# The even mixer's attention output made by feature: values stand in the array, GpSimd scales the probabilities

## The reference, cut to what matters

```python
def even_mixer(x, w_in, w_uk, w_uv, b_f, w_o, rel_bias):
    ...
    # latent heads (a): keys chosen by the indexer, at most 128 of those up to the query
    la = einsum('bthr,btkr->bhtk', ql, c_sel) + bias
    pa = jax.nn.softmax(la, axis=-1)
    oa = einsum('bhtk,btkr->bthr', pa, c_sel)
    ...
    # forgetting heads (b)
    lb = einsum('bthd,bshd->bhts', qb, k_b) + cum_f(query) - cum_f(key)
    pb = jax.nn.softmax(where(causal, lb, -inf), axis=-1)
    ob = einsum('bhts,bshd->bthd', pb, v_b)
    ...
    o_a = einsum('bshr,hrd->bshd', oa, w_uv).reshape(bsz, seq, 512)
    return concatenate([o_a, ob], axis=-1) @ w_o
```

## Time and profile before

| | us |
|---|---|
| median of 3 runs | 1915.85 (1915.56 to 1916.55) |
| the profiled execution | 1915.55, its span 1913.5 |
| TensorE busy | 1871.7 (98%) |
| VectorE, ScalarE, GpSimd busy | 928.1, 727.5, 386.2 |
| even mixer, units under way | about 772 to 952 |

### The profile page before, as it was taken

How to read it: one execution, slowest core, us unless ns; L and a number is a source line. 1 busy time by engine, 2 the same in 40 slices (tenths; PEclk the granted TensorE clock), 3 DMA queues, 4 the chain that set the end, 5 groups by cost and what they waited for, 6 DMA issues and landing times.

```text
span 1913.5 us, 23337 instructions
## 1 busy us (share of the span) xinstructions
PE 1871.7 (98%) x9766; PEld 1543.6 (81%) x9766; DVE 928.1 (49%) x1501; ACT 727.5 (38%) x1223; POOL 386.2 (20%) x224
## 2 busy tenths in 40 slices
PE   7999988999999999999999999999989999999998
PEld 6788977888888888777788888888768898888886
DVE  5675544322322234776555555523543366556334
ACT  5664434322322243556734334321323244344211
POOL 1433433111110034211031111100254421111000
PEclk9999989999999999999999999999999999999999
DMA  5211032232233232110022322332322322322321
GB/s 198 69 53 67 7 120 81 88 103 95 90 109 110 80 136 69 67 42 26 23 82 95 101 98 89 118 113 78 110 88 87 112 78 99 108 91 91 119 99 66
DMA packets 28764, 170.01 MB, mean 89 GB/s; under 512 B 3386, under 2 KB 5602, under 8 KB 10866
## 3 DMA queue, kind: packets, MB, share of 16 engines
q1 hardware_dynamic: 28660, 168.53, 25.4%
HBM read 166.37 MB, written 2.11 MB: 88 GB/s over the span
## 4 chain that ended last, share of the span: by engine, by line
PE 93%; DVE 3%; ACT 2%; POOL 1%; issue 0%; DMA 0%; SPq 0%; ACTq 0%; DVEq 0%
PE ps L572 27%; PE ps L573 27%; PE ps L574 27%; PE ps L1112 2%; PE ps L1040 1%; PE ps L1075 1%; PE ps L1079 1%; PE ps L1097 1%; POOL wL L2494 1%; PE ps L652 1%; ACT wH L1281 1%; PE ps L702 1%; PE ps L856 0%; PE ps L865 0%; DVE hL L1819 0%; PE ps L1051 0%
## 5 line engine op out<-in xcount | busy, mean ns | idle before, releaser
L572 PE MATMUL ps<-hH,wH 128*128 128x512 f32 (+1 forms) x1568 | 603.3, 385 | 5.4 <-POOL wL L2494 1.9
L574 PE MATMUL ps<-hH,wL 128*128 128x512 f32 (+1 forms) x1568 | 591.1, 377 | 0.0
L573 PE MATMUL ps<-hL,wH 128*128 128x512 f32 (+1 forms) x1568 | 591.0, 377 | 0.0
L1812 DVE TENSOR_TENSOR wL<-raw,wH 128x1024 fp32r<-128x1024 f32 (+1 forms) x196 | 240.3, 1265 | 331.5 <-ACT wH L1281 331.5
L1281 ACT ACTIVATE wH<-raw 128x1024 fp32r<-128x1024 f32 (+2 forms) x298 | 290.2, 1023 | 282.5 <-PE ps L574 282.5
L2494 POOL TENSOR_TENSOR wL<-raw,wH 128x1024 fp32r<-128x1024 f32 (+2 forms) x102 | 246.4, 2438 | 689.8 <-ACT wH L1281 689.8
L572 PEld LDWEIGHTS ps<-hH,wH 128*128 128x128 f32 x1568 | 296.1, 189 | 66.6 <-issue 5.5
L574 PEld LDWEIGHTS ps<-hH,wL 128*128 128x128 f32 x1568 | 295.8, 189 | 54.4
L573 PEld LDWEIGHTS ps<-hL,wH 128*128 128x128 f32 x1568 | 296.1, 189 | 52.3 <-issue 1.4
L572 PE MATMUL ps<-wH,aH 128*128 128x512 f32 x528 | 209.0, 396 | 0.0
L574 PE MATMUL ps<-wH,aL 128*128 128x512 f32 x528 | 208.8, 395 | 0.0
(11 more groups left out here) (370 smaller groups left out, 1918.8 us busy)
## 6 DMA issues: line engine op xcount, KB each, us to landing
raw<-in_wbig SPq DMA_DIRECT2D x139, 1024.0 KB, 4.8
rows<-in_rows SPq DMA_DIRECT2D x12, 512.0 KB, 5.8
x<-in_x SPq DMA_DIRECT2D x8, 512.0 KB, 5.7
raw<-in_wbig SPq DMA_DIRECT2D x8, 512.0 KB, 3.6
out<-x SPq DMA_DIRECT2D x4, 512.0 KB, 2.6
near<-u_scratch SPq DMA_DIRECT2D x1, 1024.0 KB, 7.3
raw<-in_wbig SPq DMA_DIRECT2D x1, 1000.0 KB, 8.1
raw<-in_wbig SPq DMA_DIRECT2D x1, 600.0 KB, 10.7
```

Of the source, the lines that this page charges most:

```text
L572: e.matmul(o, hi, m_hi, start=first, stop=False)
L573: e.matmul(o, hi, m_lo, start=False, stop=False)
L574: return e.matmul(o, lo, m_hi, start=False, stop=end)
L1812: e.tensor_tensor(wL[r][:, cs], raw[r][:, cs], wH[r][:, cs].bitcast(F32), ALU.subtract).then_inc(*low_dve.one(c, h))
```

## The change

The value product is turned round: the 64 columns of values stand in the array, and the 128 queries of a block of `Pt` are streamed. Its result has the features of one head on 64 partitions (the lower half for even heads, the upper for odd ones) and the queries along the columns. ScalarE copies it without a scale to `oTb` or `oTa`, which already have the layout of `hH`. The scale, one number a query, is now applied before the transpose: VectorE's reciprocal follows its exponential in the same iteration, and GpSimd multiplies the probabilities by it (a new strand `units` on GpSimd), and the transpose waits for that. No transposes of the output are left. Seven of its eight tiles are rounded and subtracted in seven F steps (`OUT_TILES`), the eighth, tile 3, in four parts during the output product. The order string is another one. On VectorE the wait for the earlier unit's output copy before a score's maximum is gone, and GpSimd's copies for the indexer come one step later.

```diff
 def even_order():
-    return ("FFFFFIFFFFFFFFFFFFFFFFFFFFFIFFFFFFFFFFFFFFFFIFFFFFFFIFIFFIFIFIFIFIFIFFFIFFIIFFIIIIFFFFIIFFFFIFIIFAFIFFFIIIFFIFFIAFAFFAIA"
-            "AAAIAAFAIAAIAFAFIAIFFIAIFAAAAFFAAIAAFIAAIFAAIAAIAIFAIFAAAFAIFIFAIFFFFIIAAIAIAFFIAFAFAAIFFAAIAAIAFFAIFFIAFIAFAIAAFAFIAFAI"
-            "AFAIAIIAAFAAIFIFFAIAAFFIAAAFFFFFAAFFIAIAAAFIAAFIAIFFIFAAIAAAFIIAAFAFIAFAAAAIAAIAFIAAIFAIAAFIAAAAAIAAAAAIAAAFAAAAIAAAAAFI"
-            "AFAAFAIAAAAIAAAAAAAFAFIAAAAFAIAAAAAIAAAAIAAAAAAAAAAIAAAAAAAAAAIAAAAAAAFAAAAFAAAFAAFA")
+    return ("FFFFFFFFFFFFFFFFFFFFFFFFFIFFFFFFFFIFFFFFFFFFIFFFFFFFIFIFIFIFIFIFIFIIFFIFFFFIIIFFFFFIFFFIIFIFIIFFFAFIFIAFAFIFIFAAIIFFAIFF"
+            "FAIFAAIAFAAIAAAIFAIAAIIFAAFFFFAFAIIAAAIAAIAFAAFFAIAFAIIAFFAAFIAIAAIIAFFIFAAFAFFAIIIIFFIAFIAAFIFAIAAIAAIAAIAAFFAIAIAFFAFI"
+            "AAAIFAAAIFAFFIAFIFFAFFAFIAIFFAAAAIAAFAFAIAFFAAIAFAAIFIAAFIIIIFAFIAAAFFAIFFAIAAAIAAIAAIAAIFAAFAAIAAAAAAAAIAAFFAAIAAAAAAAA"
+            "AIAFFAIAAAAAAAAAAIAFFAAIAAAAAAAAIFAAAIAAAAAAIAAAFAIAAIAAAAAAFAAAAAAAAAAAAAAAAAAFAAFFAFF")
...
         cf = R("cf", [8, 2, 512])
-        otb = R("otb", [128, 4, 512])
+        oTb = R("oTb", [128, 4, 512])
         sco = R("sco", [128, 512])
...
         va = R("va", [128, 4, 512])
-        ota = R("ota", [128, 4, 512])
+        oTa = R("oTa", [128, 4, 512])
         sel_at = [0, 0, 256, 640]
...
             "row", "x_again", "ones_q", "ones_k", "CM", "wuk", "wuv", "anti", "far", "near", "cum_q", "cum_k", "sgg", "sgw", "sgb", "out")}
-        pre, ev, gate, att, ssd, gdn0, gdn1, sums, mix, res, ffn, even, idx, unit, lat, odd, sgu, ln = stages = [
+        pre, ev, gate, att, ssd, gdn0, gdn1, sums, mix, res, ffn, even, idx, unit, lat, heads, odd, sgu, ln = stages = [
             Marks(sem, n) for n in ("pre", "evac", "gate", "att", "ssd", "gdn0", "gdn1", "sums", "mix", "res", "ffn", "even", "index",
-                                    "unit", "latent", "odd", "sgu", "norm")]
+                                    "unit", "latent", "heads", "odd", "sgu", "norm")]
         gdn = (gdn0, gdn1)
...
-            def turn_b(i):
-                turn("mix", i, otb[:, i, :], [unit.act.at("o", 28 + i)], (1,), i % 2)
-            def turn_a(i):
-                turn("mix", i, ota[:, i, :], [unit.act.at("o", 60 + i)], (0,), 4 + i)
             def dense_even():
...
                     yield from feat(C_QA + j, [0, 1], "res", lambda t: [even.act.at("qa", 2 * j + t)])
-                for i in range(4):
-                    turn_b(i)
+                for k in OUT_TILES:
                     yield
...
                         clear(b)
-                        w.wait_ge(*unit.act.at("exp", n + 1))
+                        w.wait_ge(*unit.pool.at("scaled", n + 1))
                         for j in range(i + 1):
...
                         for j in range(i + 1):
-                            t = e.matmul(ps[6][:, 0:64], Pt[n % 2][:, 128 * j:128 * j + 128], v[:, j, 64 * h:64 * h + 64], start=j == 0, stop=j == i)
+                            t = e.matmul(ps[6][64 * (h % 2):64 * (h % 2) + 64, 0:128], v[:, j, 64 * h:64 * h + 64], Pt[n % 2][:, 128 * j:128 * j + 128], start=j == 0, stop=j == i)
                         t.then_inc(*unit.pe.one("o", n))
...
             def of_mixed(k, i):
-                return [turned_lo.at("mix", i, k // 4)]
-            turn3 = ln_stage(0, [63, 64], [65, 66], hH, hL, of_mixed, True, {i: lambda i=i: turn_a(i) for i in range(4)})
+                return [heads.dve.at("last", i) if k == 3 else heads.dve.at("lo", k)]
+            turn3 = ln_stage(0, [63, 64], [65, 66], hH, hL, of_mixed)
             conv_ffn(0, turn3)
...
         def conv_start(n):
-            return [sgu.dve.at("lo", 7)] if n else [turned_pe.at("mix", 3, 0)]
+            return [sgu.dve.at("lo", 7)] if n else [heads.dve.at("last", 3)]
+        OUT_TILES = [4, 5, 6, 7, 0, 1, 2]
+        def oT(k):
+            return (oTa if k < 4 else oTb)[:, k % 4, :]
+        def out_unit(k):
+            return (32 if k < 4 else 0) + 8 * (k % 4) + 7
...
-            if tag == "mix":
-                return [prod.at(62, 1)]
             return {"first": [], "xn": [prod.at(16, i)], "res": [prod.at(50, i)], ("ln", 0): [prod.at(66, i)],
...
                         yield from feat_side(c, split, even_tile(c))
-                for i in range(4):
-                    turn("mix", i, (1,), i % 2)
-                    yield
-                yield "done"
+                for k in OUT_TILES:
+                    w.wait_ge(*prod.at(62, 1))
+                    w.wait_ge(*unit.act.at("o", out_unit(k)))
+                    e.activation(hH[:, k, :], oT(k), ACT.Copy).then_inc(*heads.act.one("hi", k))
+                    yield
+                yield "done"
+            def last_high(i):
+                w.wait_ge(*prod.at(62, 1))
+                w.wait_ge(*unit.act.at("o", 60 + i))
+                e.activation(hH[:, 3, 128 * i:128 * i + 128], oT(3)[:, 128 * i:128 * i + 128], ACT.Copy).then_inc(*heads.act.one("last", i))
...
                         h, i = n % 32 // 4, n % 4
+                        r = slice(64 * (h % 2), 64 * (h % 2) + 64)
                         w.wait_ge(*unit.pe.at("o", n))
-                        w.wait_ge(*unit.dve.at("rec", n))
                         if n >= 32:
                             w.wait_ge(*unit.pe.at("score", 31))
-                        o = ota if n >= 32 else otb
-                        e.activation(o[:, i, 64 * h:64 * h + 64], ps[6][:, 0:64], ACT.Copy, scale=sx2[:, n % 4, 2:3]).then_inc(*unit.act.one("o", n))
+                        o = oTa if n >= 32 else oTb
+                        e.activation(o[r, h // 2, 128 * i:128 * i + 128], ps[6][r, 0:128], ACT.Copy).then_inc(*unit.act.one("o", n))
                         yield
...
-            turn3 = ln_stage(0, [63, 64], [65, 66], True, {i: lambda i=i: turn("mix", i, (0,), 4 + i) for i in range(4)})
+            turn3 = ln_stage(0, [63, 64], [65, 66], True, {i: lambda i=i: last_high(i) for i in range(4)})
             conv_ffn(0, turn3)
...
                         yield from feat_side(c, split, even_tile(c))
-                for i in range(4):
-                    turn("mix", i, (1,), i % 2)
-                    yield
-                yield "done"
+                for k in OUT_TILES:
+                    w.wait_ge(*heads.act.at("hi", k))
+                    e.tensor_tensor(hL[:, k, :], oT(k), hH[:, k, :].bitcast(F32), ALU.subtract).then_inc(*heads.dve.one("lo", k))
+                    yield
+                yield "done"
+            def last_low(i):
+                s = slice(128 * i, 128 * i + 128)
+                w.wait_ge(*heads.act.at("last", i))
+                e.tensor_tensor(hL[:, 3, s], oT(3)[:, s], hH[:, 3, s].bitcast(F32), ALU.subtract).then_inc(*heads.dve.one("last", i))
...
                         w.wait_ge(*unit.pe.at("score", u))
-                        for p in [idx.pe.at("widx"), idx.act.at("ln"), idx.dve.at("negcum")] if u < 4 else [unit.pe.at("turn", u - 4), unit.act.at("o", u - 4)]:
+                        for p in [idx.pe.at("widx"), idx.act.at("ln"), idx.dve.at("negcum")] if u < 4 else [unit.pe.at("turn", u - 4)]:
                             w.wait_ge(*p)
...
                         yield
+                    if 0 <= n + 2 < 64:
+                        s = (n + 2) % 4
+                        w.wait_ge(*unit.act.at("exp", n + 2))
+                        e.reciprocal(sx2[:, s, 2:3], sx2[:, s, 1:2]).then_inc(*unit.dve.one("rec", n + 2))
                     if 0 <= n + 1 < 64:
-                        s = (n + 1) % 4
-                        w.wait_ge(*unit.act.at("exp", n + 1))
-                        e.reciprocal(sx2[:, s, 2:3], sx2[:, s, 1:2]).then_inc(*unit.dve.one("rec", n + 1))
                         yield
...
-            turn3 = ln_stage(0, [63, 64], [65, 66], True, {i: lambda i=i: turn("mix", i, (0,), 4 + i) for i in range(4)})
+            turn3 = ln_stage(0, [63, 64], [65, 66], True, {i: lambda i=i: last_low(i) for i in range(4)})
             conv_ffn(0, turn3)
...
                         yield from feat_side(c, split, none)
-                for i in range(4):
+                for k in OUT_TILES:
                     yield
...
             def index():
-                for _ in range(3 + 72):
+                for _ in range(3 + 72 + 1):
                     yield
...
                         e.tensor_copy(mb[r][:, mb_at[i]:mb_at[i] + n], selm[:, sel_at[i]:sel_at[i] + n]).then_inc(*(lat.pool.one("far") if (r, i) == (1, 3) else lat.pool.one()))
-                for _ in range(1 + 20):
-                    yield
+                for _ in range(20):
+                    yield
+                yield "done"
+            def units():
+                for n in range(-3, 64):
+                    if n + 3 < 64:
+                        yield
+                    if 0 <= n + 2 < 64:
+                        s, wd = (n + 2) % 4, 128 * ((n + 2) % 4 + 1)
+                        w.wait_ge(*unit.dve.at("rec", n + 2))
```

(9 more changed lines are left out.)

## The result

The changed kernel takes 1934.08 us (median of 4, 1933.60 to 1935.33) against 1915.70 (1913.69 to 1916.55) for the kernel before: a ratio of 1.0099, 95% interval 1.0086 to 1.0112. It is 18.4 us slower, where 1934.0 was predicted. The profiled execution ran 1933.6 us, its span 1931.1.

The account below looks back on a forecast made before the run. TensorE's own instructions bound the kernel; +18.7 for borders, +1.6 for passes, -3.5 for transposes and +1.5 for the last units made +18.3 on 1915.6, so 1934 us, with 1926 to 1943 holding 8 in 10.

Parts of the forecast that it names:

- passes of 128 columns: Value product in the even mixer: 320 passes at 0.109 us each make 34.9 us, +1.6 us.
- transposes removed: 32 transposes of the output leave TensorE's path: -3.5 us.
- What binds: Even mixer: TensorE is busy throughout, so each nanosecond its instructions take more or less moves the end as much.
- The border term: Value products in the even mixer: changes between full-array and half-array form rise from 64 to 175, +18.7 us.
- The waits: Last units of the even mixer: the longer chain makes units 59 and 63 late, +1.5 us, from 0 to 4.
- GpSimd's price: GpSimd's product of probabilities and 1/sum: 1.04 us for 512 columns, about 0.3, 0.55, 0.8 for smaller ones, 43 us.
- The middle costs nothing: Even mixer before the last units: other TensorE work covers the longer chain from exponential to transpose, so nothing is booked.
- the GpSimd rival: Last 32 units and chunk starts: late GpSimd products or a held-up reciprocal delay transposes, 15 us more, 1949; chance 0.13.
- The borders cost nothing: At the 63 visits of value products the drain is covered, leaving 1915.2 us; chance 0.05.
- The halves run side by side: Value products overlap in both array halves, saving 17 us: about 1898 with borders unpaid, 1917 with them paid; chance 0.02.
- 0.32 us after a dense product: Sign in the profile after: a value product starts 0.32 us after a dense product, where 0.23 stood.
- The loader idle by "issue" on both sides: Sign in the profile after: the weight loader is idle before and after each value-product visit, by "issue".

Follow-up runs that it names:

- the cleanest pair of runs: The changed kernel without GpSimd's product, once with values at full width and once at half width: 1917.45 us and 1932.95 us.
- the full-width form: The changed kernel with all 128 columns of values of two heads standing in the array: 1920.55 us; under the old order string 1958.13 us.
- halves and pairs: The changed kernel with the same values in both array halves, 64 queries through each, and two units' value products back to back: 1931.20 us.

## Why the prediction was right, step by step

**The total** was right to 0.1 us, and that is luck: two terms are off by -1.4 and +2.3 us and partly cancel, and the four executions of the changed kernel alone differ by 1.7 us. The sum's terms against what the stages show (+21.0 in the mixer and -1.9 in the output stage, +19.1 in all, where +18.3 was predicted):

| term | predicted | measured |
|---|---|---|
| 111 more borders | +18.7 | +17.3 (0.156 us each) |
| passes of 128 columns | +1.6 | +1.6 (0.108 to 0.109 a pass) |
| transposes removed | -3.5 | about -3.7 (1.9 in the output stage; the rest taken as equal) |
| more idle time of TensorE | +1.5 | +3.8 |
| not assigned | 0 | about +0.1 |

**What binds** was right: TensorE's own instructions, start to start. Of 21 us in the mixer, 3.8 are idle time.

**The border term** had its mechanism and its count right (111 more, 175 in all, as in the trace) and its size some 7% too high: 0.156 us each from the cleanest pair of runs, where 18.7 / 111 = 0.168 was taken. The four pairs of runs give 0.146 to 0.164. The visit at 900.64 costs 0.10 on the way in and 0.14 on the way out, plus about 0.03 for the score after it, 0.27 in all, where the prediction booked 0.34 for such a visit. Line 1178, from which its 0.35 came, is followed by a dense product, most value products by a score, and I had priced that exit (0.20) for all alike. The mean visit costs 2 x 0.156 = 0.31, so others cost more than this one; I did not price the kinds one by one.

**The waits** were under-sized, which errs the other way: +1.5 booked, +3.8 measured. GpSimd's share is what I named: 2.3 us, twice, in the last units. In the timeline of the second:

```profile
964.38 0.69 DVE L2335 CUSTOM_DVE_ANT_0 rows<-ps,mb 128x512 f32<-128x512 f32 x1 [1.36 <-PE ps L1072]
...
965.19 0.15 DVE L2342 RECIPROCAL sx<-sx 128x1 f32<-128x1 f32 x1
...
965.42 2.01 POOL L2660 TENSOR_TENSOR rows<-rows,sx 128x384 f32<-128x384 f32 x2 [1.70 <-DVE sx L2342]
...
966.30 0.55 PE L1090 MATMUL ps<-ident,rows 128*128 128x128 f32 x3 [1.37 <-POOL rows L2660]
```

It came at units 58 and 62, of three blocks, and not at 59 and 63 as I had put it: the reciprocal waited behind the maximum of the last score, of 512 columns. The 1.3 us at the indexer is the step that I had not made at all. I read the new order string only for which steps stand side by side on TensorE, and not for what it does to the indexer's own chain; the kernel before under this string has the same wait.

**GpSimd's price** was right: 1040 ns for 512 columns against 1.04 us from the earlier trace rows, and 399, 612 and 847 for the others (0.3, 0.55 and 0.8 taken), 46 us instead of 43. The slope from 128 to 512 columns is 214 ns for each 128, over a fixed part of about 185.

**The middle costs nothing**: right, but for a reason that I had understated. I wrote that 8 to 10 us of other work lie before the chunks' first transposes and 4.4 us or more between a score and its transpose. That is a property of the new string. Under the old one the full-width form waits 28 us for GpSimd, with nearly the same count of steps. The changed kernel itself, at half width, was not run under the old order. So the mechanism of the GpSimd rival (0.13, 1949 us) is real, and it comes out under an order that differs little to the eye. It is worth 43 us there, more than the 15 that I gave it: 28 us of waits, and a granted clock that falls as well.

**The other rivals.** "The borders cost nothing" falls: without them 1920.55, with them 1934.08. "The halves run side by side" does not happen in the change, as argued (all passes of a unit go to one half), but the mechanism holds wherever both halves are fed. The Trainium skill (TensorEngine Tiling (Array Packing), When to Use Tiling) recommends standing values and column tiling for a narrow streamed side. The runs bear out only what the halves do to the passes when both are in use: two passes of 64 columns take 0.058 us together, where one of 128 takes 0.109. No form with standing values and column tiling was faster here than the kernel before: +7.2 us with both halves in use, +18.4 with one, +16.3 with halves and pairs; and with the full array it was +4.6.

**The marks that I had set.** 0.32 us after a dense product: 0.33. The loader idle by "issue" on both sides: yes. The stage some 20 us longer: 21.0. TensorE's waits by GpSimd of 1 to 3 us: 2.3.

**Two sums** of the prediction are off by a little, and nothing hangs on them. By its own price of 18.7 us for 0.35 us a visit, the borders' cost is within 0.2% below 0.08 us a visit, not 0.09, and its terms at their upper ends come to about 1939, not 1941.

## What to carry to other kernels

Before a product is put into half of TensorE's array, count the visits and ask who fills the other half in the same visit: here a border costs 0.15 to 0.16 us and is paid by the visit, while the gain of the halves, 0.05 us for each pair of passes, is paid by the pass and only if both halves work. By these numbers, an estimate, a visit with both halves in use pays off from about six pairs on (0.31 / 0.05). Visits of two to eight pairs, five on average, cost 2.9 us in the kernel before, and visits of ten pairs on average gained 2.7. With one half in use it never did, and the full array, with results that nobody reads, was cheaper. And when a change puts an engine into the chain of a tightly woven schedule, look at which instruction stands ahead of it in each queue that the chain now crosses: the same operations cost 2 us under one order and 43 under another.

## What the runs showed of the hardware that I had not expected

- Two passes of 64 streamed columns in the two halves of the array take 0.058 us together. They do the work of one pass of 64 columns in the full array, which takes 0.11 (0.22 us for each block more, of two passes), or of one of 128 columns in one half, which takes 0.109. In a visit of one block the two borders cost more than this gives (0.27 us instead of 0.17, and 0.10 before it for the way in); in one of four blocks it wins (0.62 and 0.10 instead of 0.84).
- 128 streamed columns in full array and in half array cost the same within 3% (0.112 and 0.109 us a pass), so half width in itself gains nothing.
- Idle time of TensorE can cost more than itself. With 28.6 us idle in 284, in waits of up to 3.4 us, the mean granted clock was 0.96, about 11 us more; with 16.7 us idle it was 0.97; with 0.2 to 5.5 it was 0.99 to 1.00. At full width, with 5.3 us idle, it fell once, after waits of 1.5 and 0.2 us; with full width in the latent heads alone and 5.4 us idle it did not. Which waits bring the clock down I did not settle.
